# A layer boundary cut into column halves: last product, scatters, row loads, combines, splits, first weight steps

## The reference

```
for l in range(DEPTH):                     # DEPTH = 2
    [u|q|k|v|g] = rmsnorm(x) @ w_in[l]     # 1024 -> 2560
    x = x + concat(pool_mix(u), silu(g) * groupnorm(retention(q, k, v))) @ w_out[l]
    h = rmsnorm(x)
    # top-1 of 4 expert groups, then top-2 of its 4 experts: gates (rows, 16), two of them not zero
    y = sum over e of ((silu(h @ w_gate[e]) * (h @ w_up[e])) * gates[:, e]) @ w_down[e]
    x = x + y
y_out = rmsnorm(x)
```

## Time and profile before

| | |
|---|---|
| median of 3 runs | 861.51 us |
| profiled execution, its own time | 858.05 us |
| its span, first to last instruction | 856.3 us |
| PE busy | 830.1 us (97%) |
| DVE busy | 601.2 us (70%) |
| ACT busy | 479.1 us (56%) |
| POOL busy | 296.4 us (35%) |
| mean granted clock | 0.995 |

### The profile page before, as it was taken

How to read it: one execution, slowest core, us unless ns; L and a number is a source line. 1 busy time by engine, 2 the same in 40 slices (tenths; PEclk the granted TensorE clock), 3 DMA queues, 4 the chain that set the end, 5 groups by cost and what they waited for, 6 DMA issues and landing times.

```text
span 856.3 us, 12142 instructions
## 1 busy us (share of the span) xinstructions
PE 830.1 (97%) x4187; PEld 664.7 (78%) x4187; DVE 601.2 (70%) x945; ACT 479.1 (56%) x817; POOL 296.4 (35%) x199
## 2 busy tenths in 40 slices
PE   8999999999999999999899999999999999999994
PEld 5788788898867888888478888888888678888851
DVE  4435546655688999998654454656647799999956
ACT  3633342612467888887544333352335598888863
POOL 0014993301031677321000199703101337752110
PEclk9999999999999999999999999999999999999998
DMA  8622223323948999996864222322377599999839
GB/s 291 177 75 82 74 62 98 100 62 93 411 141 307 405 355 394 392 364 197 293 175 142 82 73 62 96 65 62 96 297 315 159 415 353 380 385 386 322 120 322
DMA packets 73055, 185.82 MB, mean 217 GB/s; under 512 B 15885, under 2 KB 30733, under 8 KB 64667
## 3 DMA queue, kind: packets, MB, share of 16 engines
q1 hardware_dynamic: 59034, 153.33, 50.8%
q0 software_dynamic: 10368, 23.09, 7.8%
q10 hardware_dynamic: 3600, 8.73, 2.8%
HBM read 170.63 MB, written 29.39 MB: 234 GB/s over the span
## 4 chain that ended last, share of the span: by engine, by line
PE 83%; DVE 8%; DMA 4%; ACT 2%; issue 1%; SPq 1%; POOLq 0%; ACTq 0%; DVEq 0%
PE ps L422 14%; PE ps L426 11%; PE ps L425 11%; PE ps L1283 10%; PE ps L1285 9%; PE ps L1284 9%; PE ps L1290 3%; PE ps L424 3%; PE ps L1484 2%; PE ps L1261 1%; DMA hg<-xn_d,rowidx 1%; DVE x L1987 1%; PE ps L1424 1%; DMA back<-y_d 1%; PE ps L1449 1%
## 5 line engine op out<-in xcount | busy, mean ns | idle before, releaser
L422 PE MATMUL ps<-wh,hT 128*128 128x512 f32 x480 | 194.0, 404 | 3.5 <-DVE lT L1803 2.8
L1888 DVE TENSOR_TENSOR gul<-wgu,eh 128x1024 fp32r<-128x1024 f32 x128 | 150.6, 1216 | 4.0 <-ACT eh L994 3.6
L426 PE MATMUL ps<-wh,lT 128*128 128x512 f32 x384 | 150.1, 391 | 0.0
L425 PE MATMUL ps<-wl,hT 128*128 128x512 f32 x384 | 150.0, 391 | 0.0
L784 POOL DMA_INDIRECT y_d<-y,rowidx x32 | 100.5, 3142 | 123.0 <-DVE y L1908 120.8
L994 ACT ACTIVATE eh<-wgu 128x1024 fp32r<-128x1024 f32 x128 | 128.9, 1057 | 9.2 <-PE ps L1285 5.0
L1879 DVE SCALAR_TENSOR_TENSOR wl<-raw,gcol,wh 128x512 fp32r<-128x512 f32 x80 | 76.1, 956 | 81.8 <-ACT wh L967 81.7
L422 PEld LDWEIGHTS ps<-wh,hT 128*128 128x128 f32 x480 | 90.3, 188 | 25.4 <-DVE lT L1803 5.4
L1283 PE MATMUL ps<-eh,hgTh 128*128 128x512 f32 x240 | 96.5, 402 | 0.4 <-issue 0.4
L967 ACT ACTIVATE wh<-raw,gcol 128x512 fp32r<-128x512 f32 x80 | 57.4, 722 | 66.7 <-PE ps L424 50.2
L1285 PE MATMUL ps<-eh,hgTl 128*128 128x512 f32 x240 | 94.0, 392 | 0.0
(11 more groups left out here) (227 smaller groups left out, 1544.3 us busy)
## 6 DMA issues: line engine op xcount, KB each, us to landing
wgu<-in_gate_up SPq DMA_DIRECT2D x64, 1024.0 KB, 13.4
wdn<-in_w_down SPq DMA_DIRECT2D x64, 512.0 KB, 14.0
raw<-in_w_in SPq DMA_DIRECT2D x80, 256.0 KB, 2.7
raw<-in_w_out SPq DMA_DIRECT2D x32, 256.0 KB, 3.0
back<-y_d SPq DMA_DIRECT2D x14, 512.0 KB, 7.4
s<-in_state_ret POOLq DMA_DIRECT2D x8, 512.0 KB, 5.3
xn_d<-xf ACTq DMA_DIRECT2D x8, 512.0 KB, 6.0
x<-in_x_prompt SPq DMA_DIRECT2D x4, 512.0 KB, 6.3
```

Of the source, the lines that this page charges most:

```text
L422: pe.matmul(out, both, w_h, start=first, stop=False)
L425: pe.matmul(out, both, w_l, start=False, stop=False)
L426: return pe.matmul(out, l[:, t * P:(t + 1) * P], w_h, start=False, stop=final)
L1888: ve.tensor_tensor(gu_pair(gul, gul3, e, s, p), gu_pair(wgu, wgu3, e, s, p), gu_split(e, p)[:, :].bitcast(F32), ALU.subtract).then_inc(glo, 1)
```

## The change

The boundary is worked in halves of the 1024 columns. (1) The down product of expert 15 makes bank 0 completely before bank 1 and signals each; ACT copies bank 0 as soon as it is there. Both weight splits for it are placed before the Silu. (2) Its scatter becomes two of 512 columns. (3) SP loads the rows by half and tile, both picks in one DMA (`pair`), five for the first halves and five for the second; ACT loads none at this boundary. (4) `combine_half` adds the two picks of a half with two instructions. (5) PE makes the four early weight steps, which use only the first halves, over all tiles before most second halves are transposed (`halves_first`); transposes, `mix_hi` and `mix_lo` are numbered first halves first. Weight step 4 (the first of the second half) is made tile by tile behind them, and its weight splits move into that order. (6) `end_mask(L, 0)` moves behind the last evacuation, `end_mask(L, 1)` ahead of the three `w_hi`; 25 idle turns of PE become 14, and 6 become 3. The end of the kernel after layer 1 keeps its full rows, but has the new down product, scatters and mask order.

```diff
@@ sync
+            def row_halves(L):
+                by_row = y_d.rearrange("(k r) d -> r k d", k=2)
+                for half in range(2):
+                    if half == 0:
+                        sp.wait_ge(y_sc[0], 16 * YUSES[0] * (L + 1))
+                        sp.wait_ge(y_sc[1], 16 * (YUSES[1] * (L + 1) - 1))
+                        sp.wait_ge(y_sc[2], 16 * YUSES[2] * (L + 1))
+                    else:
+                        sp.wait_ge(y_sc[1], 16 * YUSES[1] * (L + 1))
+                    cols = slice(512 * half, 512 * half + 512)
+                    for t in range(NT):
+                        n = tokens(t)
+                        sp.dma_start(pair[t][0:n, :, cols], by_row[t * P:t * P + n, :, cols]).then_inc(
+                            row_ld[t] if half == 0 else second_ld if t < 2 else third_ld, 16)
...
                     for s in range(RAW, EARLY[L + 1]):
                         load_raw(L + 1, s)
+                if L + 1 < NL:
+                    row_halves(L)
+                    continue
@@ gpsimd, scatter
+                if final(e):
+                    by_half = y_d.rearrange("r (h d) -> (r h) d", h=2)
+                    pool.wait_ge(y_sc[1], 16 * (YUSES[1] * (L + 1) - 1))
+                    for half in range(2):
+                        pool.wait_ge(yV if half else yA, NE * L + e + 1)
+                        pool.indirect_dma_start(out=by_half, ...,
+                                                in_=y[s][:, 512 * half:512 * half + 512], ...).then_inc(y_sc[half], 16)
+                    return
@@ scalar, expert
-                if not final(e):
+                if final(e):
+                    dn_hi(L, e, s, n[1])
+                else:
                     gu_hi(L, e + 1, (s + 1) % 3, n[2], range(2 if first(e) else 0, 3))
                 sc.wait_ge(gpe, X * 4 + 4)
                 sc.activation(act[:, :], gu_bank(e)[:, 0:F], ACT.Silu).then_inc(silu_done, 1)
...
                 if final(e):
-                    dn_hi(L, e, s, n[1], (1,))
                     y_evac(L, e - 1, (s + 2) % 3, n[0])
-                    end_mask(L, 0)
@@ scalar, layer 1
+                    for t in range(NT):
+                        mix_hi(L, t, (0,))
+                    for t in range(3):
+                        mix_hi(L, t, (1,))
+                    w_hi(L, EARLY[L])
+                    for t in (3, LAST):
+                        mix_hi(L, t, (1,))
@@ scalar, after the experts
                 y_evac(L, NE - 1, (NE - 1) % 3, (NE - 1) // 3)
+                end_mask(L, 0)
...
                 sc.wait_ge(dpe, 2 * NE * (L + 1))
+                end_mask(L, 1)
                 if L + 1 < NL:
                     for s in range(RAW):
                         w_hi(L + 1, s)
-                end_mask(L, 1)
@@ tensor
+            def halves_first(L):
+                mix_rows(L, 0, (0,))
+                idle_turns(0, 3)
+                pe.wait_ge(hi_done, 15 * L + 1)
...
+                mix_rows(L, 1, (0,))
+                pe.wait_ge(lo_done, 15 * L + 1)
...
+                for t in range(1, NT):
+                    pe.wait_ge(lo_done, 15 * L + t + 1)
+                    for s in range(EARLY[L]):
+                        win_mm(L, s, t)
+                        if s == 1 and t + 1 < NT:
+                            mix_rows(L, t + 1, (0,))
+                    if t >= 3:
+                        mix_rows(L, t - 3, (1,))
+                mix_rows(L, 2, (1,))
+                mix_rows(L, 3, (1,))
+                for t in range(NT):
+                    pe.wait_ge(lo_done, 15 * L + NT + t + 1)
+                    win_mm(L, EARLY[L], t)
+                    if t == 0:
+                        mix_rows(L, LAST, (1,))
...
                 if L + 1 < NL:
                     end_state(L, 0)
-                    idle_turns(0, 10)
                     end_state(L, 1)
-                    idle_turns(0, 15)
+                    idle_turns(0, 14)
@@ vector
+            def combine_half(L, t, half):
...
+                for k in range(2):
+                    if k:
+                        ve.wait_ge(comb, COMBS * L + 2 * turn(L + 1, t, half) + 1)
+                    ve.scalar_tensor_tensor(out=x[0:n, t, cols], in0=pair[t][0:n, k, cols], scalar=pgate[0:n, k, t:t + 1], in1=x[0:n, t, cols],
+                                            op0=ALU.mult, op1=ALU.add).then_inc(comb, 1)
@@ vector, layer 1
+                    w_lo(L, 0)
+                    sample_state(L - 1, 0)
+                    w_lo(L, 1)
+                    sample_state(L - 1, 1)
+                    w_lo(L, 2)
+                    combine_half(L - 1, 0, 0)
+                    w_lo(L, 3)
+                    combine_half(L - 1, 1, 0)
+                    for t in range(2, NT):
+                        mix_lo(L, t - 2, (0,))
+                        combine_half(L - 1, t, 0)
+                    mix_lo(L, 3, (0,))
+                    combine_half(L - 1, 0, 1)
+                    mix_lo(L, LAST, (0,))
+                    combine_half(L - 1, 1, 1)
+                    combine_half(L - 1, 2, 1)
+                    mix_lo(L, 0, (1,))
+                    combine_half(L - 1, 3, 1)
+                    mix_lo(L, 1, (1,))
+                    combine_half(L - 1, LAST, 1)
+                    mix_lo(L, 2, (1,))
+                    w_lo(L, EARLY[L])
+                    mix_lo(L, 3, (1,))
+                    mix_lo(L, LAST, (1,))
```

More of the change, by code:

```diff
@@ L208, in build @@
         back = [tile(f"back{i}", [P, D], off=shared + 4096 * i) for i in range(2 * NT)]
+        pair = [tile(f"pair{t}", [P, 2, D], off=shared + 8192 * t) for t in range(NT)]
         r12 = place(12 * 1024)
@@ L1037, in expert @@
                 sc.activation(act[:, :], gu_bank(e)[:, 0:F], ACT.Silu).then_inc(silu_done, 1)
[L1038 to L1040 removed]
+                if not final(e):
                     rows_hi(L, e + 1)
@@ L1627, in _ @@
                 experts(pe, lambda e, s, n: expert(L, e, s, n))
-                for k in range(2):
-                    down(L, NE - 1, (NE - 1) % 3, k)
+                down_last(L)
                 idle_turns(0, 4)
@@ L1913, in expert @@
                     dn_lo(L, e - 1, (s + 2) % 3)
-                if not final(e):
+                if final(e):
+                    dn_lo(L, e, s)
+                else:
                     gu_lo(L, e + 1, (s + 1) % 3, range(3))
```

157 lines of the change are left out of this document (82 added, 75 removed).

## The result

| | before | after |
|---|---|---|
| median, 12 runs each on one chip | 860.87 us (857.76 to 862.12) | 862.85 us (860.39 to 867.41) |
| profiled execution, its own time | 858.05 us | 862.03 us |
| span | 856.3 us | 860.2 us |
| mean granted clock | 0.995 | 0.987 |

The ratio of the runs is 1.004, 95% interval [1.0024, 1.0056]: the change costs 3.4 us (2.1 to 4.8). It was forecast as slower by 0.5%, and it is slower by 0.4%. The two profiled executions lie 3.98 us apart, where the sum had +4.3. The ratio is not the quotient of the two medians, which would be 1.0023.

The account below looks back on a forecast made before the run. PE bounds the kernel, so layer 1 moves with step 7: +4.7 us there and -0.4 at the end make +4.3, 862.4 profiled; 3.5 more for the median of the runs gives 865.8, range 862.0 to 869.0.

Parts of the forecast that it names:

- the sum: Whole kernel: step 7 of layer 1 +4.7 us, end of kernel -0.4, together +4.3 us; chance 0.62.
- both chains of the forecast: Ahead of step 7: chunk 5's split behind the squares, and small tables delaying chunk 7; both give about 456.9.
- the low case: Rival at the boundary: small terms all come out low, +2.0 us, 863.2, counted as no difference; chance 0.13.
- my own range: Range of the sum, 864.3 to 867.3: rows landing 417.5 to 419.5, end -0.85 to +0.3.
- The load ends last: Before the first combine: row load lands at 418.3, after VectorE is free at 417.8, so the combine starts at 418.3.
- The queue step: SP at the boundary: moved masks delay chunk 3's load to 414.2; row loads follow at 414.5, before 413.93.
- cost nothing while the clock holds: PE's idle turns, 25 to 14 and 6 to 3: they fill idle time, so cutting them costs nothing at held clock.
- the fall as a rival: PE's clock falls at the boundary: step 4 and its transposes slow, +1.7 us, 867.5; chance 0.15.
- The pair gap: VectorE's half combines: second term starts 0.1 us after the first ends, a tile half costs 1.51, ten 15.1.
- three signs: Wrong if row loads went out at 412, VectorE never idled in first halves, or second terms started without gap.
- The branch between the masks: ScalarE at the boundary: a branch of 0.4 to 0.6 us between mask h = 0 and mask h = 1.
- Without that cover it would eat the 0.4: Kernel end: ScalarE's later row load lands about 835.7, needed at 836.0, so hidden; otherwise it eats the 0.4 us gain.

Follow-up runs that it names:

- e4_w4_tables: e3_w4 with small tables issued behind chunk 7's load and weight split 5 ahead of ScalarE's squares; ratio to the kernel before 1.0033.
- e12_hold: e4_w4_tables with ten idle turns (six and four) in PE's waits for the last halves ahead of step 4; ratio to the kernel before 1.0061.
- e14_free: e12_hold with its small tables back ahead of chunk 7's load and without their wait for the last combine; ratio to the kernel before 1.0002.
- e1_masks: The changed kernel with the second head mask put back behind the three weight splits; ratio to the kernel before 1.0077.
- e8_turns: The changed kernel with the idle turns of before (10 and 15, and 6 for 3); ratio to the kernel before 1.0045.
- e9_start_turns: e5_start with idle turns of 10 between the state products and 8 behind them; ratio to the kernel before 1.0043.
- e5_start: e1_masks with VectorE's second state update moved behind two half combines; ratio to the kernel before 1.0064.
- e3_w4: The changed kernel with VectorE's low split of weight chunk 4 put ahead of the last combine; ratio to the kernel before 1.0056.
- e11_before_cut: The kernel before with the idle turns of the change (0 and 14); ratio to the kernel before 1.0008.
- e15_before_free: The kernel before with layer 1's small tables no longer waiting for the last combine; ratio to the kernel before 1.0012.

## Why the prediction came out as it did

| step of the prediction | forecast | trace after |
|---|---|---|
| row loads out | 414.5 | 413.71 |
| first half combine | 418.3 | 417.62 |
| first product | 421.4 | 421.39 |
| from tile to tile | 3.7 | 3.51 (425.37, 428.88, 432.40) |
| last combine ends | 443.3 | 442.34 |
| step 4 | 444.6 | 443.75 |
| step 5 | 450.5 | 450.18 |
| low split of chunk 7 ends | 456.7 | 456.48 |
| step 7 | 456.9 | 456.70 |
| the end, against before | -0.4 | -0.60 |

**The sum held.** Step 7 lies 4.48 us later than before (forecast +4.7), the rest is the same (372.67 and 372.65), and from the last down product to the end of the span it takes 30.83 us instead of 31.43. That is 4.48 + 0.02 - 0.60 = +3.90, and the spans differ by 3.9. Counted from t0, step 7 is 4.91 later, where the forecast comes to 4.8; layer 0 ended 0.28 earlier in this execution than forecast, and that is chance. The mechanism is in the main the forecast one: VectorE, in order, idle in the first halves; two instructions for each half combine; then the split of chunk 4 behind the last combine, chunk 5 behind the squares, and the small tables behind the last combine.

**Where it was luck.** The first product came at 421.39 as forecast (421.4) by two errors: the half row of tile 0 was complete at 419.15 and not at 419.9, and the 14 turns at the lower clock gave that back. Step 5 is alike. The last combine and with it step 4 came almost 1 us earlier than forecast, but from step 4 to step 5 it took 6.43 us where the forecast had 5.9. e4_w4_tables, with split 5 ahead of the squares, needs 5.78, and e12_hold, at full clock besides, 4.44. So the slow clock is worth 1.3 us in this stretch and the squares 0.7, and the forecast had it all without the clock. Three ends met here. PE's own products, with the slow step 4 among them, and split 5 were ready for step 5 within 0.1 us of each other: the chain of waits names the products, but step 5 starts 0.34 us behind its predecessor, where 0.23 is usual. Chunk 7's split was there 0.22 us before step 7. So both chains of the forecast are there, with a third beside them that it did not have, and each hides much of what the others cost.

**The level was off.** The forecast of 865.8 is 3 us above the measured median. 0.6 of it is the base: 12 runs of before have their median at 860.87, the three shown had 861.51. The medians differ by 1.98 and the ratio says 3.4, against the +4.3 forecast. The single traces differ by 3.98, but that of before lies 2.8 us under its median and that of after 0.8, so they do not settle the level. The change's runs spread over 7 us, and those of highest clock are the shortest (0.993: 860.39; 0.982: 867.41): how much of the time the clock was down differs from run to run. Two of my sums were also off: the low case, +2.0 on 861.51, is 863.5 and not 863.2, so it lay above the edge to slower and not on it, and the bounds named for my own range give 864.5 to 867.7 and not 864.3 to 867.3.

**"The load ends last" was wrong.** That step took the later of two numbers half a microsecond apart (418.3 for the load, 417.8 for VectorE), and the first was at least 0.7 us too late and the second 0.2. The first combine at 417.62 waited for nothing but VectorE's order. It was a near tie that other traces of the same start decide the other way (0.41 us of waiting for the load in e4_w4_tables, 0.65 in e14_free). The queue step before it was right, and of no effect: e1_masks brought the loads forward by 1.3 us and lost by its edit, since the mask that it put back feeds the state update. I had priced the masks only for what is queued on ScalarE and SP behind them, not for the one state update of VectorE that needs them.

**Idle turns "cost nothing while the clock holds" hid the wrong case.** The clock did not hold. It fell near 412 (granted 0.97 in the four microseconds before, 0.50 in the four behind), after PE had done four turns and four state products with holes of 0.86 and 0.39 us since 407.7, busy 2.75 of the 4 us. I had the fall as a rival with 0.15 and priced only step 4. Its condition was met, its price was not: the low split of chunk 7, which SP's tables set, ended at 456.48, so without the slow step 4 the time would have been only about 0.2 us shorter (an estimate from that row). Where the fall did cost was in a place that I had not priced, the 14 turns that stand ahead of the first transposes (0.4 us by e8_turns; 4.9 at the first product in e9_start_turns against e5_start, with six turns fewer in it). The Trainium skill, page "TensorE: Matmul & The Clock Gate" (section "A second HAM failure mode: psum-queue depth-cycling"), tells of one kernel in which short pauses of PE between groups of products came often enough for the clock to go down and up again. The trace after agrees, with holes of 0.86 and 0.39 us, and e14_free shows that such holes need not bring it down: holes of 0.86 and 0.38 us, granted 1.00. I had weighed only the rule on an idle array.

**Small terms.** The pair gap of 0.1 does not exist: two dependent half combines take 1.45 from start to next start, four take 2.98, and ten of them are 0.6 us less than my 15.1. That was one of the three signs that I had named for being wrong; the other two did not come. The branch between the masks did not show (16 activations in 4.77 us): 0.5 of the 0.8 us by which the row loads came earlier than forecast, the rest being the earlier end of layer 0. At the first product nothing of it was left. From there the loop of 3.51 instead of 3.7 gave 0.7 and the missing gap 0.2, together the 0.95 us of the last combine. At step 7 only 0.2 was left: on the chain of the tables because they took 9.7 us of issuing (442.38 to 452.08) instead of the 9.0 of the earlier trace rows, and on PE's because of the clock.

**The end.** The half scatter did not give 0.8: its rows are there 3.29 us after its issue (831.03 to 834.32) against 3.54, and counted from the last product 4.95 against 5.28. The first combine started 0.53 earlier than before counted from there. But the second one waited 0.71 us for ScalarE's row load, sent at 834.86 behind the moved mask. This is the cover of which I had said "Without that cover it would eat the 0.4": the load needed 6.12 us from issue, and it was not hidden. So nothing of the 0.53 arrived: the last store went out 27.14 us behind the last down product, before 27.09. The end is 0.60 shorter because that store took 3.69 us to the end of the span instead of 4.34, which no part of the change explains. The forecast amount was met by luck.

## What to carry to other kernels

Before cutting a stage in halves to start it earlier, write down for every engine that works in order what stands behind the first halves: an earlier start is worth only what the last full piece, and the loads and small transfers released by it, come earlier. When two chains end together, mending one shows nothing, so judge an edit by its marker in the trace and only then by the time. Filler that holds the clock must stand where its worst length, at the lower clock, still ends before the next real input is there, and between the products whose holes it is to close.

## What the runs showed of the hardware

- The granted clock fell to 0.50 (412 to 416 in the trace after) although PE had not idled for more than 0.86 us at once in the four microseconds before; e3_w4, e4_w4_tables and e12_hold show the same holes and a fall. In e14_free the same instructions with the same holes ran at 1.00, and the clock fell some 8 us later, counted from t0 (0.61 from 424 to 428), behind a wait of 2.22 us. With ten turns between the products it stayed at 1.00 in all six traces. In e11_before_cut the hole was 2.69 us, and the clock 0.86 and 0.71.
- A scatter of half the bytes saved 0.25 us of 3.54 from issue to rows there (at the end of the kernel, one of each). Two in place of one cost POOL 0.98 each.
- One issue of a small table (the broadcast bias) took 4.74 us on SP in the trace after and 1.56 in e15_before_free, where instead the first of the nine took 4.89 (0.43 in the trace after). The nine together took 9.7 us after the combines and 11.9 sent early, where nobody waited for them.
- A row load of ScalarE's queue beside nine of SP's needed 6.12 us from issue to landing when it went out 0.54 us behind SP's first; at the same place in the kernel before, sent together with SP's first, it needed 5.0.
